# GpSimd makes the low parts of the later stages' weights in four operations instead of one

## What is computed

```python
proj = h @ w_in                       # first block, recurrence: streams, scan, readout
y = (y + bonus) * silu(g) @ w_out
proj = h @ w_in                       # differential attention, 8 pairs of heads
attn = softmax(q1 k1) - lam * softmax(q2 k2);  y = rms_norm(attn @ v) * silu(g) @ w_out
proj = rms_norm(x) @ w_in_2[l]        # two layers: causal, dilated and memory attention
x = x + (softmax(q k) @ v * silu(g)) @ w_out_2[l]
```

## Time and profile before

| | us |
|---|---|
| median of three runs | 2569.64 |
| lowest, highest | 2568.6, 2583.72 |
| the profiled execution, as a run | 2575.68 |
| its span, first to last instruction | 2573.9 |
| TensorE busy with matmuls | 2209.8 |
| DVE busy | 1367.8 |
| ACT busy | 1156.6 |
| GpSimd busy | 679.5 |

### The profile page before, as it was taken

One profiled execution on the slowest core, in us unless ns is written; L12 is line 12 of the kernel. 1 busy time (PEld: TensorE's weight loads), 2 busy tenths in 40 slices (PEclk: granted clock), 3 DMA queues, 4 the chain that ended last, 5 costly groups with the idle time before them and its releaser, 6 DMA issues.

```text
span 2573.9 us, 59035 instructions
## 1 busy us (share of the span) xinstructions
PE 2209.8 (86%) x25736; PEld 1631.9 (63%) x25736; DVE 1367.8 (53%) x2342; ACT 1156.6 (45%) x1933; POOL 679.5 (26%) x410
## 2 busy tenths in 40 slices
PE   8799999288888878876879999996899988899978
PEld 2587777167766767765667666654666665566656
DVE  1367878334444545454346566653456653466652
ACT  2466666233333334333244555453355553354552
POOL 0334453300011011013133222223433432433332
PEclk9899999599998999998889999997999998999998
DMA  7116362733332222214121111102111111111121
GB/s 269 64 50 184 117 184 84 209 113 106 84 95 79 59 75 57 61 38 159 58 87 60 34 42 40 50 25 83 59 65 50 58 58 66 66 58 58 50 66 66
DMA packets 148482, 211.32 MB, mean 82 GB/s; under 512 B 81921, under 2 KB 106753, under 8 KB 147457
## 3 DMA queue, kind: packets, MB, share of 16 engines
q1 hardware_dynamic: 137120, 164.28, 20.2%
q0 software_dynamic: 9952, 40.11, 5.1%
q10 hardware_dynamic: 1152, 3.15, 0.3%
HBM read 165.30 MB, written 42.21 MB: 81 GB/s over the span
## 4 chain that ended last, share of the span: by engine, by line
PE 62%; DVE 15%; ACT 11%; issue 7%; POOL 3%; DMA 2%; SPq 0%; ACTq 0%; DVEq 0%; POOLq 0%
PE ps L258 9%; PE ps L260 8%; PE ps L259 8%; PE ps L1332 3%; PE ps L538 3%; PE ps L1322 2%; PE ps L1347 2%; PE ps L2233 2%; PE ps L391 2%; PE ps L2729 2%; PE ps L2706 1%; DVE st L2292 1%; PE ps L311 1%; PE ps L1197 1%; DVE s L916 1%
## 5 line engine op out<-in xcount | busy, mean ns | idle before, releaser
L243 POOL TENSOR_TENSOR wbl<-wb,wbh 128x1024 fp32r<-128x1024 f32 x128 | 315.8, 2467 | 595.9 <-ACT wbh L238 591.1
L258 PE MATMUL ps<-hTh,wah 128*128 128x512 f32 (+1 forms) x512 | 181.0, 353 | 17.4 <-POOL wal L243 11.0
L258 PE MATMUL ps<-hT2h,wbh 128*128 128x512 f32 x416 | 181.5, 436 | 16.3 <-POOL wbl L243 8.9
L258 PE MATMUL ps<-hT1h,wbh 128*128 128x512 f32 (+1 forms) x432 | 176.5, 409 | 3.1 <-POOL hT1l L2372 3.1
L259 PE MATMUL ps<-hTl,wah 128*128 128x512 f32 (+1 forms) x512 | 175.1, 342 | 0.0
L260 PE MATMUL ps<-hTh,wal 128*128 128x512 f32 (+1 forms) x512 | 174.9, 342 | 0.0
L339 POOL TENSOR_TENSOR ro<-ro 128x256 f32<-128x256 f32 (+1 forms) x12 | 11.9, 993 | 582.9 <-DVE ro L323 582.9
L238 ACT ACTIVATE wbh<-wb 128x1024 fp32r<-128x1024 f32 x128 | 134.6, 1052 | 69.4 <-PE ps L1928 43.5
L260 PE MATMUL ps<-hT2h,wbl 128*128 128x512 f32 x416 | 164.2, 395 | 0.0
L259 PE MATMUL ps<-hT2l,wbh 128*128 128x512 f32 x416 | 163.8, 394 | 0.0
L243 POOL TENSOR_TENSOR wal<-wa,wah 128x1024 fp32r<-128x1024 f32 x34 | 102.1, 3004 | 219.7 <-ACT wah L238 219.7
(11 more groups left out here) (400 smaller groups left out, 5676.6 us busy)
## 6 DMA issues: line engine op xcount, KB each, us to landing
wb<-in_w_in SPq DMA_DIRECT2D x56, 512.0 KB, 3.4
s_str_dram<-s POOLq DMA_DIRECT2D x48, 576.0 KB, 8.7
wm<-in_ada SPq DMA_DIRECT2D x48, 512.0 KB, 4.6
bkv<-s_str_dram SPq DMA_DIRECT2D x96, 192.0 KB, 3.3
wa<-in_rw_in SPq DMA_DIRECT2D x34, 512.0 KB, 3.5
wb<-in_da_in SPq DMA_DIRECT2D x32, 512.0 KB, 3.4
ARI<-s_str_dram SPq DMA_DIRECT2D x96, 128.0 KB, 3.5
wb<-in_w_out SPq DMA_DIRECT2D x16, 512.0 KB, 3.4
```

The source lines that it names most:

```text
L243: e.tensor_tensor(self.lo[:, n % 2], self.raw[:, n % 3], self.hi[:, n % 2].bitcast(F32), ALU.subtract).then_inc(self.K.s.w_lo, 1)
L258: e.matmul(z, wh[:, k, :], hi[:, k, a:b], start=k == 0, stop=False)
```

## The change

The class gets a number of pieces, and `split_lo` makes the low part in that many operations, each over 8 / pieces of the eight groups of 128 columns. The ring wb of the later stages is made with four pieces: four operations of 128x256, back to back, with no wait between them. The semaphore w_lo goes up with the last of them. The ring wa of the first stage keeps one operation.

```diff
-    def __init__(self, K, c, name, plan):
-        self.K, self.plan = K, plan
+    def __init__(self, K, c, name, plan, pieces=1):
+        self.K, self.plan, self.pieces = K, plan, pieces
...
             e.wait_ge(self.K.s.w_hi, self.hi0 + n + 1)
-            e.tensor_tensor(self.lo[:, n % 2], self.raw[:, n % 3], self.hi[:, n % 2].bitcast(F32),
-                            ALU.subtract).then_inc(self.K.s.w_lo, 1)
+            w = 8 // self.pieces
+            for k in range(0, 8, w):
+                i = e.tensor_tensor(self.lo[:, n % 2, k:k + w, :], self.raw[:, n % 3, k:k + w, :],
+                                    self.hi[:, n % 2, k:k + w, :].bitcast(F32), ALU.subtract)
+            i.then_inc(self.K.s.w_lo, 1)
...
-        W = Weights(K, ctx, "wb", plan)
+        W = Weights(K, ctx, "wb", plan, 4)
```

## The result

| | before | changed |
|---|---|---|
| median of 17 runs each, us | 2574.25 | 2586.47 |
| lowest, highest | 2567.32, 2583.72 | 2580.37, 2596.69 |
| profiled execution's span | 2573.9 | 2583.7 |
| mean granted clock of TensorE in it | 0.936 | 0.937 |

The account below looks back on a forecast made before the run. TensorE was taken to bound the kernel, paying only where it waits for the low part. Terms 5.3 + 1.9 + 2.9 + 0.8 + 2.4 - 2.0 - 0.2 = +11.1 us on 2569.64 gave 2581 us, range 2570 to 2594.

Parts of the forecast that it names:

- The bound: TensorE, busy 86% of the span; a later low part costs only where TensorE waits, 20 blocks plus two near.
- the way through GpSimd's queue in the six heads: First attention layer: a later split delays L2359, which holds DVE's L332 0.4 us longer; +2.4 us over six heads.
- Step (1): The split itself: four pieces take 2.77 us, +0.4 us for each block, 51 us more GpSimd time.
- Step (2): DVE operations between pieces: +0.53 us at each of ten steady gates, 5.3; blocks 50 and 90, 1.9.
- Blocks 50 and 90: First pair of heads: DVE's L332 runs before the last piece, split ends 0.95 us later, twice, 1.9 us.
- rival C: Clock: longer stops bring half clock to all 20 gates, 27 us on top, 2608 us; chance 0.04.
- Step (3): Other gates, blocks 2, 42, 45, 75, 77, 85, 115, 117: +0.3 or +0.4 us each, sum 2.9 us.
- step (5): DVE's relief: L2790 in the two last layers, -2.0 us net; L2308 in the first attention layer, -0.2 us.
- Step (4): GpSimd steps queued behind splits: +0.8 us in the middle stage, +2.4 us in six first-attention-layer heads.
- A (DVE's relief pays): Rival: earlier DVE shortens TensorE's ten steady waits for L2790, gain 13.8 us, result 2567; chance 0.08.
- B (no handover): Rival: the pieces keep the port, DVE is blocked 0.4 us longer; sum +11.5 us, 2581; chance 0.07.
- D: Rival: pieces cost 1.0 us each, gates 1.6, steady blocks gate too; 2605 us or more; chance 0.04.

Follow-up runs that it names:

- the lateness alone: Kernel before, split kept whole, plus a 128x128 subtraction into an unread buffer that alone raises w_lo: 2585.89 us beside 2575.41, ratio 1.0039.
- pieces used as they come: Changed kernel with every piece raising w_lo and products waiting piece by piece, all blocks in four: 2567.15 us beside 2575.41 for the kernel before.
- the fastest one: Kernel before with four signalled pieces, awaited piece by piece, in the 22 gating blocks plus 15, 80 and 120: 2562.0 us beside 2574.48, ratio 0.9948.
- the gates alone: Kernel before with four pieces only in the 22 gating blocks, semaphore raised with the last piece: 2585.52 us beside 2574.48, ratio 1.0042.
- pieces and signals in the gates: Kernel before with four pieces, each signalled and awaited, only in the 22 gating blocks: 2570.85 us beside 2574.48, ratio 0.9977.
- the kernel with the relief and no gate late (the rest): Kernel before with four pieces in the 98 blocks neither gating nor ahead of queued GpSimd steps: 2571.9 us beside 2574.48, ratio 0.9991.

## Why the prediction was right, point by point

**Right.** The bound (TensorE, 20 to 22 gates), the duration of the pieces (0.73 us forecast, 737 ns measured in the median; starts 0.68 to 0.70 apart), the loss of 0.4 us for each gate, the way through GpSimd's queue in the six heads, and the handover to DVE all came as written. L2317's wait went from 1.27 us to 1.70, and the six heads cost 2.55 us where 2.4 was forecast. The sum of 11.1 stands beside 11.7 in the trace and 12.2 in the medians. Part of that closeness is luck: errors of up to 2 us in the terms cancel, and the rows of the table add up to 12.3 us, of which places that no row names take back 0.7.

**Two signs missed.** GpSimd's busy time is 757.8 us where 730 to 750 were forecast. The prediction counted what DVE puts between the pieces only at the gates; in the trace DVE's larger operations get in at 25 other blocks too and hold the split 0.9 to 1.6 us longer than one operation took, in place of 0.4. All 128 splits together take 395.5 us in place of 315.9, 80 more and not 51. It cost no time, as those blocks have margin, but that was not foreseen. And DVE's busy time fell by 37 us where 40 to 60 were forecast. The line:

```profile
L245 POOL TENSOR_TENSOR wbl<-wb,wbh x512: 718/737/1481, 1206.9 to 2572.7; 128x256 fp32r<-128x256 f32 x171
```

**Step (1), confirmed for its reason.** The added time of a split is 0.42 us, not the 0.53 that recorded durations would give: four records of 737 ns are 2.95 us, and the four take 2.82 from first start to last end. The Trainium skill (Perfetto Trace Analysis, GPSIMD Engine Instruction) has this rule, and these numbers agree with it.

**Step (2), the insert, mis-sized.** The prediction added 0.13 us to each steady gate for DVE's L2790 between the pieces. L2793 does run between them (0.69 us in place of 1.65), and the split is 0.42 to 0.43 us longer than before, no more than at block 42, where DVE is quiet (2.79 in place of 2.36): the insert cost nothing. The term was 5.3 and measured 4.2. A longer DVE step does cost: at block 50, where L332 comes in between (L335 now), the pieces take 3.3 us.

```profile
1862.25 0.69 DVE L335 SCALAR_TENSOR_TENSOR sqc<-sqc,Rc 128x512 f32<-128x512 f32 x1
...
1863.58 0.50 PE L261 MATMUL ps<-hT2h,wbh 128*128 128x512 f32 x1 [3.85 <-POOL wbl L245]
```

The stop is 3.85 us beside 2.91, 0.94 longer where 0.95 was forecast.

**Blocks 50 and 90, too small.** 1.9 forecast, 3.8 measured. The other 1.9 lies beside the stops: 0.75 ahead of the one at block 50, where the kernel before and the changed one show these windows (length, then busy time of TensorE, its weight loads, DVE, ACT and GpSimd, then the clock):

```profile
1843.80:1857.00 13.20, 13.17 (x48) 10.43 (x48) 8.00 (x8) 3.72 (x7) 5.63 (x4) 0.84 0.00 0
```

```profile
1844.20:1857.80 13.60, 13.22 (x46) 10.76 (x47) 8.32 (x9) 3.45 (x6) 5.98 (x4) 0.77 0.00 0
```

TensorE is as busy, at a clock of 0.77 in place of 0.84: the product that starts at 1844.58 runs at 0.50 for 5.9 us, before it was 4.3. The longer stop comes only behind that, so it can't be the cause, and why the low clock lasts longer there stays open. The rest is 1.15 behind the stop at block 90, where 3.3 us at a clock of 0.50 became 6.7. That is the mechanism of the prediction's rival C at a small scale: it was priced there, and kept out of the sum. It is no fixed price: behind the same stop of 3.85 us at block 50 the low clock lasted as long as before. The kernel with the lateness alone (stops of 3.78 us) loses 3.6 at these blocks too, its extra part all ahead of the stops, and the one with two pieces (3.06) loses 0.2. So it does not hang on the four pieces; whether it hangs on the length of the stop or on where the low clock happens to fall, these single executions can't tell. Where the stops shrink (pieces used as they come), the products behind them are 1.7 us faster at 51 and at 91, beside the 1.5 that the prediction read from the earlier trace rows. The first 4 us of block 50's product have a clock of 0.58 in the kernel before, and of 1.00 in the fastest one:

```profile
1861.10:1865.10 4.00, 3.98 (x11) 3.11 (x12) 1.21 (x2) 0.70 (x1) 2.69 (x1) 0.58 0.44 135
```

```profile
1856.50:1860.50 4.00, 4.00 (x15) 2.87 (x16) 2.66 (x4) 2.19 (x4) 4.00 (x4) 1.00 0.10 20
```

**Step (3), scattered.** The memory heads cost 2.2 where 2.2 was forecast (1.4 in step (3) and the two gates of 0.4 that step (5) had taken off its gain), but not as written: 75, 77, 79, 115, 117 and 119 have 0.27 to 0.33 each where 0.3 to 0.4 was, and 74, 78, 114 and 118, which I had cost at nothing, 0.10 to 0.17. 42, 45 and 85 cost 0.6 where 1.2 was: 45 and 85 have 0.4 each as forecast, and around 42 the two executions differ by 0.6 the other way for no reason that I found.

**Step (4), right in the six heads, too small in the middle stage.** Two splits ahead of L1824 were forecast as 0.8, and the step at block 1 is 1.0. But the step leaves out what block 0 itself lost. Counted from the start of the first split, block 0 starts 0.42 us later and block 1 1.44 later. Of this 0.85 is the two splits; the rest goes with a handover that the prediction did not have: the third L1824 (L1827 now) takes 2.53 us in place of 1.80, because GpSimd comes to it late enough for DVE's own low part L1881 to be in its way, and the fourth is done 1.56 us later. With eight pieces it stayed at 1.82. The third and fourth together, before and after:

```profile
1217.49 4.28 POOL L1824 TENSOR_TENSOR yTl<-yr,yTh 128x768 fp32r<-128x768 f32 x2
```

```profile
1215.93 5.01 POOL L1827 TENSOR_TENSOR yTl<-yr,yTh 128x768 fp32r<-128x768 f32 x2
```

Block 2, of step (3): 0.41 forecast as 0.3.

**Step (5), the relief, right in place, uncertain in size.** The wait of 1.41 us at the transposes of block 80 is gone:

```profile
2130.91 0.90 DVE L2793 TENSOR_SCALAR pc<-pc,stc 128x256 f32<-128x256 f32 x1
...
2131.86 0.44 PE L2718 MATMUL ps<-con,pc 128*128 128x128 f32 x2
```

At that matmul the changed kernel had won back 1.5 us since the start of block 79, but by the start of block 80 only 0.50. In between, TensorE's next scores take longer in the changed kernel, here the rows of before and after:

```profile
2137.69 0.71 PE L2706 MATMUL ps<-kc,qc 64*128 64x256 f32 x4 [3.15 <-ACT pc L2747]
```

```profile
2141.95 1.23 PE L2709 MATMUL ps<-kc,qc 64*128 64x256 f32 x4 [3.16 <-ACT pc L2750]
```

and the windows over the whole stretch have a granted clock of 0.68 where the kernel before has 0.74 (it is 0.50 for 16.9 us there, before for 13.6):

```profile
2127.50:2154.00 26.50, 18.49 (x73) 9.70 (x74) 12.72 (x45) 9.16 (x26) 1.26 (x1) 0.74 0.00 1
```

```profile
2131.80:2158.50 26.70, 18.79 (x70) 9.29 (x70) 13.70 (x45) 8.81 (x25) 3.74 (x4) 0.68 0.00 0
```

The columns of the table with relief give -1.0 to -3.3 at the four blocks in question. Of those without it two (the lateness alone, the gates alone) give -1.2 and -1.7 as well, and one, pieces and signals in the gates, +5.4. Against the first two, no more than 0.4 to 0.9 of the changed kernel's -2.1 is the relief's, and the rest differs between executions. How much of it the clock takes back each time stays open.

The small relief at L2308, forecast as -0.2, is read more surely than the large one, before and after:

```profile
1397.58 3.04 DVE L2308 SCALAR_TENSOR_TENSOR p<-p,st,p 128x768 f32<-128x768 f32 x1
```

```profile
1396.20 1.37 DVE L2311 SCALAR_TENSOR_TENSOR p<-p,st,p 128x768 f32<-128x768 f32 x1
```

Block 15 comes 0.24 to 0.41 us earlier in all six kernels that cut its split, and 0.0 in the three that don't.

**The rivals.** A (DVE's relief pays) is out: the kernel with the relief and no gate late (the rest) is at 0.9991, and the sixteen waits for L2790 fell by 2.6 us of 31.5, all of it at 80 and 120. B (no handover) is out: L2632's median of 1104 ns and L2793's longest of 0.90 us show it. D is out: 0.14 us a border. C was too dear as written, with no steady gate at half clock; behind the stop at block 90 it was at work. A weak point that the prediction named, the size of the inserts, was indeed the worst of its read numbers; that the worst total error was at blocks 50 and 90 it had not said.

## What to carry to other kernels

Cutting an operation that others wait for makes its end later by a fixed amount for each border, and that is paid wherever a consumer stands at the gate; it gains only if the consumer is also let in piece by piece. So cut where it is waited for, signal each piece, and leave the rest whole: here four pieces with four signals in 25 of 128 blocks turned 12.2 us lost into 12.5 us won. By the medians 3.6 us of that came with the gates alone, and 9 with the three blocks whose cutting frees a DVE step. And count a relief by the waits of the bounding engine that end on the relieved one: 37 us off DVE was worth one or two at most, until TensorE came early enough to stand at the same place.

## What the runs showed of the hardware

- A GpSimd subtraction of 1, 2, 4 or 8 back-to-back parts takes 2.40, 2.54, 2.82, 3.38 us for the same 128x1024: 0.14 us for each instruction added, to 0.01 us, where no large DVE operation gets in.
- A waiting DVE operation gets its turn between two GpSimd instructions that stand back to back. DVE's 128x512 multiplication of two SBUF tensors fell from 2748 to 1104 ns when the instruction it waited behind was cut in four, and its 128x256 scaling from 2.53 to 0.90 us. The Trainium skill (SBUF — State Buffer, Who interferes with whom) has it of such a fast scaling that whoever issues second is blocked for the other's whole instruction; the 2.53 us before and 0.90 us after agree with that, per instruction.
- A 128x128 scaling let in between two pieces made GpSimd's four pieces no longer (0.42 to 0.43 us over one operation, with it and without). One 128x512 operation on two SBUF tensors (block 50) made them 0.5 us longer; at block 68, where two such and a scaling of 128x512 got in, they took 4.18 us.
- TensorE's clock: behind a stop of 1.41 us at block 80 the next twelve matmuls came at full clock (2.4 GHz, steps of 0.23 us), behind 0.51 us too, and behind 2.09 us at the same place eight of them at half (1.2 GHz, steps of 0.43). There 0.68 us more of waiting went with 1.6 us lost to the clock. The other traces agree at these two places: stops of 1.56 (late kernel, block 80) and 1.66 us (gates alone, block 120) were followed by a clock of 1.00, the one of 2.12 us (block 120) by 0.50.
